# Three products per weight tile, in a sequence chosen for each of six networks

## What is computed

```python
def conv_ffn(x, w_up, conv_w, conv_b, w_down):      # networks 0 and 1
    h = x @ w_up
    h = hp[:, 0:S] * conv_w[0] + hp[:, 1:S + 1] * conv_w[1] + hp[:, 2:S + 2] * conv_w[2] + conv_b
    u, g = jnp.split(h, 2, axis=-1)
    return ((u * jax.nn.gelu(g)) @ w_down).astype(x.dtype)

def swiglu(x, wg, wu, wd):                          # networks 2 to 5
    return (jax.nn.silu(x @ wg) * (x @ wu)) @ wd
```

## Time and profile before

| | us |
|---|---|
| median of three runs | 1754.56 |
| the profiled execution, its own time | 1754.94 |
| its span (first to last instruction) | 1753.1 |
| TensorE busy with matmuls | 1740.9 (99%) |
| TensorE weight loads | 1708.9 (97%) |
| VectorE busy | 1142.5 (65%) |
| ScalarE busy | 953.8 (54%) |

### The profile page before, as it was taken

One profiled execution on the slowest core, in us unless ns is written; L12 is line 12 of the kernel. 1 busy time (PEld: TensorE's weight loads), 2 busy tenths in 40 slices (PEclk: granted clock), 3 DMA queues, 4 the chain that ended last, 5 costly groups with the idle time before them and its releaser, 6 DMA issues.

```text
span 1753.1 us, 32873 instructions
## 1 busy us (share of the span) xinstructions
PE 1740.9 (99%) x14102; PEld 1708.9 (97%) x14102; DVE 1142.5 (65%) x1842; ACT 953.8 (54%) x1521; POOL 123.0 (7%) x130
## 2 busy tenths in 40 slices
PE   9999999999999999999999999999999999999998
PEld 9989999998899999999999999999999999999998
DVE  7776998575789875855547765555655556775544
ACT  7665767465467664744434454443554444764443
POOL 1002000110020002000010020001000002020003
PEclk9999999999999999999999999999999999999999
DMA  6334455545446565455554545555455554255552
GB/s 239 138 105 166 169 193 186 187 169 169 139 165 193 186 191 181 169 177 172 180 169 157 169 160 177 178 172 168 159 179 168 186 191 157 97 178 184 190 183 97
DMA packets 85057, 297.75 MB, mean 170 GB/s; under 512 B 10512, under 2 KB 13456, under 8 KB 84912
## 3 DMA queue, kind: packets, MB, share of 16 engines
q1 hardware_dynamic: 84176, 294.85, 50.3%
q10 hardware_dynamic: 736, 0.80, 0.2%
HBM read 294.57 MB, written 1.05 MB: 169 GB/s over the span
## 4 chain that ended last, share of the span: by engine, by line
PE 92%; DVE 3%; POOL 2%; ACT 1%; DMA 1%; issue 0%; SPq 0%; DVEq 0%; POOLq 0%
PE ps L1494 27%; PE ps L1493 27%; PE ps L1495 27%; PE ps L1529 2%; POOL acc L905 2%; PE ps L1524 2%; PE ps L1525 2%; DVE w_lo L932 1%; PE ps L1550 1%; PE ps L1800 1%; DMA raw<-stream 1%; DVE y L987 1%; PE ps L1504 0%; ACT w_hi L445 0%; PE ps L1820 0%
## 5 line engine op out<-in xcount | busy, mean ns | idle before, releaser
L932 DVE TENSOR_TENSOR w_lo<-raw,w_hi 128x1024 fp32r<-128x1024 f32 x557 | 691.0, 1249 | 329.4 <-ACT w_hi L445 210.7
L445 ACT ACTIVATE w_hi<-raw 128x1024 fp32r<-128x1024 f32 x557 | 580.3, 1050 | 169.8 <-DMA raw<-stream 148.0
L1493 PE MATMUL ps<-a_hi,w_hi 128*128 128x256 f32 (+1 forms) x2088 | 591.5, 283 | 0.2
L1494 PE MATMUL ps<-a_lo,w_hi 128*128 128x256 f32 (+1 forms) x2088 | 590.1, 283 | 0.0
L1495 PE MATMUL ps<-a_hi,w_lo 128*128 128x256 f32 (+1 forms) x2088 | 586.9, 281 | 0.0
L1493 PEld LDWEIGHTS ps<-a_hi,w_hi 128*128 128x128 f32 x2088 | 392.9, 188 | 1.4 <-DVE w_lo L932 0.8
L1495 PEld LDWEIGHTS ps<-a_hi,w_lo 128*128 128x128 f32 x2088 | 393.3, 188 | 0.0
L1494 PEld LDWEIGHTS ps<-a_lo,w_hi 128*128 128x128 f32 x2088 | 392.2, 188 | 0.5
L1493 PE MATMUL ps<-h_hi,w_hi 128*128 128x256 f32 (+1 forms) x1336 | 379.6, 284 | 0.2 <-DVE y L948 0.2
L1494 PE MATMUL ps<-h_lo,w_hi 128*128 128x256 f32 (+1 forms) x1336 | 378.1, 283 | 0.0
L1495 PE MATMUL ps<-h_hi,w_lo 128*128 128x256 f32 (+1 forms) x1336 | 376.9, 282 | 0.0
(11 more groups left out here) (269 smaller groups left out, 1794.7 us busy)
## 6 DMA issues: line engine op xcount, KB each, us to landing
raw<-stream SPq DMA_DIRECT2D x557, 512.0 KB, 3.3
x<-xT SPq DMA_DIRECT2D x2, 512.0 KB, 5.3
out<-x SPq DMA_DIRECT2D x8, 128.0 KB, 1.8
work<-pT ACTq DMA_DIRECT2D x2, 256.0 KB, 3.1
par<-params SPq DMA_DIRECT2D x1, 283.5 KB, 11.4
tmp<-causal ACTq DMA_DIRECT2D x1, 208.0 KB, 2.5
con<-consts SPq DMA_DIRECT2D x1, 194.5 KB, 8.8
tmp<-pos SPq DMA_DIRECT2D x1, 128.0 KB, 8.7
```

What stands on the lines that cost most here:

```text
L445: nc.scalar.activation(w_hi[:, u % SLOTS, :], raw[:, u % SLOTS, :], ACT.Copy).then_inc(w_hi_ready, 1)
L932: nc.vector.tensor_tensor(w_lo[:, u % SLOTS, :], raw[:, u % SLOTS, :], w_hi[:, u % SLOTS, :].bitcast(F32), ALU.subtract).then_inc(w_lo_rea ...
L1493: nc.tensor.matmul(dst, wh, xh, start=first, stop=False, skip_group_check=True)
L1494: nc.tensor.matmul(dst, wh, xl, start=False, stop=False, skip_group_check=True)
```

## The change

`three` takes an order as an argument, by default the one of before ("hlw"). `whole` takes two orders, for even and odd tiles k; `down` likewise for even and odd q. A new body `by_parts` takes one product for all 8 tiles of a unit before the next product, and in `down` the by-parts form does so for the four tiles q of one input tile. Two tables say which network uses which.

```diff
+UP_BY_PARTS = (1, 2)
+UP_ORDERS = {0: ("hlw", "hlw"), 3: ("hwl", "lhw"), 4: ("hwl", "lhw"), 5: ("hwl", "hwl")}
+DOWN_BY_PARTS = (0, 2)
+DOWN_ORDERS = {1: ("hwl", "lhw"), 3: ("hwl", "lhw"), 4: ("hwl", "hwl"), 5: ("lhw", "lhw")}
...
-            def three(dst, wh, wl, xh, xl, first, last):
-
-                nc.tensor.matmul(dst, wh, xh, start=first, stop=False, skip_group_check=True)
-                nc.tensor.matmul(dst, wh, xl, start=False, stop=False, skip_group_check=True)
-                return nc.tensor.matmul(dst, wl, xh, start=False, stop=last, skip_group_check=True)
+            def three(dst, wh, wl, xh, xl, first, last, order="hlw"):
+
+                for i, c in enumerate(order):
+                    ins = nc.tensor.matmul(dst, wl if c == "w" else wh, xl if c == "l" else xh, start=first and i == 0,
+                                           stop=last and i == 2, skip_group_check=True)
+                return ins
+
+            def one(c, dst, wh, wl, xh, xl, first, last):
+
+                return nc.tensor.matmul(dst, wl if c == "w" else wh, xl if c == "l" else xh, start=first, stop=last,
+                                        skip_group_check=True)
...
+            def by_parts(cw, src_hi, src_lo):
+
+                def body(u, slot, i, j, r):
+                    pe.wait_ge(w_lo_ready, u + 1)
+                    for c in "hlw":
+                        for k in range(KD):
+                            ins = one(c, ps[:, slot % BANKS, 0:cw.stop - cw.start], *tile(u, k), src_hi[:, k, cw], src_lo[:, k, cw],
+                                      c == "h" and k == 0, c == "w" and k == KD - 1)
                     ins.then_inc(unit_done, 1)
                 return body
...
-                    whole(cw, src_hi, src_lo)(u, u % BANKS, i, i // 2, i % BANKS)
+                    if f in UP_BY_PARTS:
+                        by_parts(cw, src_hi, src_lo)(u, u % BANKS, i, i // 2, i % BANKS)
+                    else:
+                        whole(cw, src_hi, src_lo, 0, UP_ORDERS[f])(u, u % BANKS, i, i // 2, i % BANKS)
...
-                            for q in range(4):
-                                ins = three(ps[:, bank + q:bank + q + 1, 0:n_cols], *tile(u, 4 * kk + q),
-                                            h_hi[:, k, cw], h_lo[:, k, cw], False, False)
+                            if f in DOWN_BY_PARTS:
+                                for c in "hwl":
+                                    for q in range(4):
+                                        ins = one(c, ps[:, bank + q:bank + q + 1, 0:n_cols], *tile(u, 4 * kk + q),
+                                                  h_hi[:, k, cw], h_lo[:, k, cw], False, False)
+                            else:
+                                for q in range(4):
+                                    ins = three(ps[:, bank + q:bank + q + 1, 0:n_cols], *tile(u, 4 * kk + q),
+                                                h_hi[:, k, cw], h_lo[:, k, cw], False, False, DOWN_ORDERS[f][q % 2])
```

6 lines of the change are left out of this document (4 added, 2 removed).

## The result

The changed kernel takes **1758.14 us** (median of 17 runs, 1757.7 to 1758.53) against 1755.28 us for the kernel before on the same chip (17 runs, 1754.02 to 1756.54). The ratio is 1.0017, with a 95% interval of 1.001 to 1.0024: slower by 2.9 us. The forecast was 1749.9 us, in a range of 1741 to 1757.5; it has the wrong sign, and the time lies outside the range. By the prediction's bound of 0.2% the loss of 0.17% is still in the middle case, to which it gave 0.40; the interval lies wholly above 1.

The account below looks back on a forecast made before the run. TensorE, 99% busy, was taken to bound the kernel through matmul count times step. Terms of -3.9 and -0.8 us, by parts at nothing, sum to -4.7 us: 1749.9 us for the median, range 1741 to 1757.5.

Parts of the forecast that it names:

- the middle case: Whole kernel's time stays within 0.2% of before; given 0.40.
- What bounds the kernel: Whole kernel: TensorE 99% busy, so time is matmul count times step; waits unchanged, other engines and queue cost nothing.
- Rhythm: Touched phases above the lowest step seen (up5 and the downs) fall to 116.67 or 125.0 ns: -3.9 us.
- Same values in a row: up3, up4, up5: h and w side by side read the same values; a quarter of 984 steps gain 3.3 ns, -0.8 us.
- By parts: up1, up2, down0, down2, one product for all tiles before the next: 0 to +2.6 us, taken as nothing.
- the sign of a loss by parts: A step in up1 above 117 ns or in up2 above 125 would put the loss on by-parts.
- A slower rhythm: Rival, touched phases: new sequences take the upper rhythm or opening's mean; +6.9 us, 1761.5, from +0.48 ns mean; chance 0.14.
- The order does not matter: Rival, all touched phases: each matmul's extra comes from reading its own values, whatever stands beside it; 1754.6 us; chance 0.36.
- A rhythm faster than any seen: Rival, touched up and down phases: 113.3 ns holds throughout, same share for 272 columns; -29 us, 1726; chance 0.12.
- The sign that the prediction itself named against the chance of a rhythm: A step in up3 or up4 moving either way by over 1 ns would show that order alone sets it.

Follow-up runs that it names:

- e5: Kernel before with one to three small 128-column matmuls ahead of some units of up0, up1, up4 and up5; 1759.36 us against 1755.97 (1.0019).
- e1: Changed kernel with order h, l, w for every tile in up and down of all six networks; 1761.84 us against 1755.54 of the kernel before (1.0041).
- e4: Changed kernel with order l, h, w in up and down of all six networks; 1761.94 us against 1755.54 of the kernel before (1.0041).
- e9: All 24 matmuls of a unit read one fixed high value tile, another in each network, order hlw; computes another sum; 1754.52 us.
- e13: Kernel before with values of 256-column phases other than up4 packed 256 apart, all 64 B from the weights' start; 1756.52 us against 1755.28 (1.0005).
- e3: Changed kernel with by parts in up and down of all six networks; 1757.20 us against 1755.54 of the kernel before (1.001).
- e17: e9 with tile 0 in all networks and a small matmul ahead of unit 20 in up0, up1 and up5; 1759.62 us.
- e12: e9 with the weights moved 64 B further on and the values 128 B; 1764.83 us.
- e10: Kernel before with tiles packed so every 256-column matmul reads values at odd multiples of 64 B from the weights' start; 1756.45 us against 1755.19 (1.0009).
- e18: Kernel before with h packed 256 apart in 256-column phases and one small matmul ahead of unit 3 of up5; 1753.51 us against 1755.42 (0.9991).
- e7: Kernel before with only 128 to 264 columns of each up unit computed, the rest left out; 1723.95 us, one execution.
- e16: e13 with single small matmuls ahead of unit 3 of up0, up1, up5, unit 43 of up1, unit 30 of up4; 1757.73 us against 1755.40 (1.0015).
- e11: The layout of e10 with the changed kernel's sequences; 1755.72 us against 1755.19 of the kernel before (1.0003).

## Why the prediction was wrong

**What bounds the kernel: right.** Only the step could matter, and only the step moved. The waits are still about what they were and the other engines are covered, so pricing them at nothing was right.

**"*Rhythm*": the step that failed.** It read 116.67 and 117.8 ns for one code in the earlier trace rows and concluded that any sequence may fall into either value, so the new ones were put at the lowest value seen, -3.9 us. The observation was right and is confirmed by e5. What was wrong is to carry it over to other sequences: e1 to e4 show one fixed step for each of them in this layout, and in up phases of 256 columns all of these (117.50, 117.78, 118.33) are above 116.67. Of the term's parts, up5 was to give -1.1 us and gave +0.5; the four downs of 256 columns were to give -2.7 and gave -0.3 (down0, down4, down5 a third of a ns or half of one lower, down1 half of one higher); up1 and up4, priced at no change, cost +0.8 and +0.9.

**"*Same values in a row*": wrong.** The gain of 0.8 us for h beside w did not come. hwl has such a pair in every triple and is, at 118.33, the slowest in 256-column up phases (e1); up3 was +0.27 ns. The streaks in the earlier trace rows were real, but what they showed, 113.3 for one tile and 118.3 for the next, is what e9 finds: reading a tile again is not enough, since two of e9's four reread tiles take 118.66 and 120.0 ns, and not needed, since e13 has 113.3 with eight tiles in turn.

**"*By parts*": the ends were right, the choice not throughout.** up1 by parts was given 0 to +1.3 us and took 0.8, where nothing was assumed; with 117.50 ns it is over the 117 that the prediction named as the sign of a loss by parts. up2 was put at nothing, and is. down0 was given -0.3 ns and got -0.5; down2 was given +0.7 to +1.5 ns and got +0.7.

**The rivals.** *A slower rhythm* was the right case, and at +6.9 us priced more than twice too high: up2's part was nothing and up3's 0.27 ns instead of 1.7. It didn't count up5, which gave +0.5. The mean over all touched steps is 2.6 us / 7296 = +0.36 ns, under its threshold of +0.48; with 17 runs of each kernel the interval excludes no change all the same. *The order does not matter* fell: e1 and e3 differ by 4.6 us with nothing else changed. *A rhythm faster than any seen* fell for this change; 113.33 ns does exist (e9), but not for these sequences in these places. The sign that the prediction itself named against the chance of a rhythm, a move of over 1 ns in up3 or up4, came true: up4 moved by 1.1 ns.

**The count.** up2 has 42 units behind its opening, not 41 (its opening takes two), so the change touches 7320 matmuls and not 7296. Nothing above moves by it.

**The odds.** Two values had been seen for hlw, the lower in most phases. Four of the five touched up phases were already at the lowest value that any whole phase had shown. That asymmetry stood in the earlier trace rows and should have put the slow side ahead of the fast one.

**What stays open.** What decides at an entry or a pause between 113.33 and 117.78 ns at 64 B from the weights. Up to the pause in up0, e9 and e17 have the same instructions on TensorE in the same order, so it lies in their timing or outside of the trace. What in the chip couples the two reads was not seen, only argued from the distance rule of e9 and e12. Nor is it known why e10's downs take 117.0 and e18's 117.8. Why the fixed steps of the other sequences are 117.50, 117.78 and 118.33 is not derived from the positions either. The times of single executions of before gather at two values about 1 us apart, which is what one up phase in the other rhythm would give (984 x 1.1 ns); with one trace for a kernel that stays an argument.

## What to carry over

Where TensorE is at 99% and a change only permutes matmuls, measure the step of every phase to a hundredth of a ns first: phases at the lowest value seen are more likely to lose than to gain, and two values for one code are a property of that code, not a reserve for another. Vary one sequence over the whole program before mixing sequences; four such runs settled here what the mixture could not tell. And when a rule found with one tile promises much (113.33 ns), test it on two more places before building a layout on it: the one built here was expected near 1725 us and came out at 1756.

## What the runs showed of the hardware

- **Position of the values against the weights.** With all else alike, 256-column matmuls with a weight load each ran at 120.0 ns where values and weights start at the same place modulo 256 B, at 118.67 at 128 B distance, and at 113.33 or 117.78 at 64 and 192 B (e9, e12, e17). With 272 columns it is 125.33 at 0 B and 126.67 at 64 and 128 B (e9, e12).
- **A floor.** 111.67 ns a matmul for 128, 192 and 224 columns (e7). TensorE: Matmul & The Clock Gate in the Trainium skill (Part 2, Back-to-back issue gap) gives about 81 ns for a sustained stream of pairs with 128 columns; the trace does not agree for this type, at 61.64 / 552 = 111.67 ns.
- **Two rhythms of one sequence, turned over by as little as one matmul.** hlw goes from 116.67 to 117.78 or back with each push of one to three small matmuls, and stays there until the next push or the end of the phase (e5, e16, e18).
- **Two rhythms with values at 64 B from the weights,** 113.33 and 117.78 ns: up0 of e9 and e17 has the same code and parts at a pause of under 0.1 us, and in e13 units of eight tiles show both. A small matmul pushed in turned none of the 117.78 over (e16, e17).
- **One rhythm only in the other sequences, in the layout of before,** as far as seen: their step is the same to 0.01 ns in networks that lie a thousand us apart (e1 to e4). They were not pushed. In the layout of e11, hwl ran at 116.67 in up5.
